# Gated one-hot rows of the PEER gates: from VectorE and ScalarE to GpSimd

## What is computed

```python
q = (xt @ w_query).reshape(T, PEER_HEADS, 2, HALF_Q)
scores = jnp.einsum('thpc,hpnc->thpn', q, sub_keys)
top_s, top_i = lax.top_k(scores, PEER_TOPK)
# the best 16 of the 16 x 16 sums of both halves: idx = i0 * 128 + i1
gate = jax.nn.softmax(best_s, axis=-1)
act = jax.nn.gelu(jnp.einsum('cd,ced->ce', xc, expert_u[ic]), approximate=False)
y = jnp.einsum('ce,ced->cd', gc * act, expert_v[ic])
```

## Time and profile before

| | |
|---|---|
| median of three runs | 3446.96 us (3443.82 to 3449.16) |
| profiled execution | 3449.76 us |
| its span | 3447.9 us |
| mean granted TensorE clock | 0.947 |
| instructions | 51796 |
| HBM read | 663.03 MB |

### The profile page before, as it was taken

One profiled execution on the slowest core, in us unless ns is written; L12 is line 12 of the kernel. 1 busy time (PEld: TensorE's weight loads), 2 busy tenths in 40 slices (PEclk: granted clock), 3 DMA queues, 4 the chain that ended last, 5 costly groups with the idle time before them and its releaser, 6 DMA issues.

```text
span 3447.9 us, 51796 instructions
## 1 busy us (share of the span) xinstructions
PE 3063.0 (89%) x18029; PEld 2438.0 (71%) x18029; DVE 1839.0 (53%) x3381; ACT 1275.3 (37%) x2062; POOL 38.0 (1%) x77
## 2 busy tenths in 40 slices
PE   6979997997999776999996999988699999689997
PEld 4763443783444756999985788877599999568885
DVE  3532222624221465697459555556559944975555
ACT  0111111021111362444447545436344444655443
POOL 0000000000000100000000000010000000000000
PEclk9989998997999868999999999987799999999998
DMA  8647996653999311445540455532135545025552
GB/s 338 269 171 295 421 421 268 256 219 136 421 421 376 112 49 74 170 174 181 182 146 0 159 185 191 183 122 101 49 135 183 183 176 183 19 100 192 183 185 95
DMA packets 91679, 665.76 MB, mean 193 GB/s; under 512 B 10336, under 2 KB 10336, under 8 KB 10656
## 3 DMA queue, kind: packets, MB, share of 16 engines
q1 hardware_dynamic: 90864, 660.65, 50.0%
q0 software_dynamic: 544, 2.42, 0.2%
q10 hardware_dynamic: 144, 1.05, 0.1%
HBM read 663.03 MB, written 1.05 MB: 193 GB/s over the span
## 4 chain that ended last, share of the span: by engine, by line
PE 73%; DVE 12%; DMA 7%; issue 4%; ACT 2%; DVEq 2%; SPq 0%; ACTq 0%
PE acc L549 21%; PE lin L549 18%; PE duo L549 9%; DMA arena<-w_moe 7%; PE lin L510 6%; PE lin L723 5%; PE duo L754 3%; DVE arena L1922 3%; PE duo L499 2%; PE duo L510 2%; PE acc L768 2%; DVE hot L1915 1%; PE acc L583 1%; DVE w_lo L1335 1%; DMA arena<-w_ada 1%
## 5 line engine op out<-in xcount | busy, mean ns | idle before, releaser
L1335 DVE TENSOR_TENSOR w_lo<-slot,w_hi 128x1024 fp32r<-128x1024 f32 x608 | 742.3, 1223 | 384.6 <-ACT w_hi L1001 381.3
L1001 ACT ACTIVATE w_hi<-slot 128x1024 fp32r<-128x1024 f32 x608 | 643.4, 1059 | 623.1 <-PE acc L549 353.5
L549 PE MATMUL lin<-x_parts,w_hi 128*128 128x256 f32 x3584 | 477.0, 286 | 74.1 <-DVE x_parts L1665 74.1
L549 PE MATMUL acc<-w_hi,x_parts 128*128 128x512 f32 x2048 | 521.6, 397 | 1.6 <-ACT x_parts L1004 1.6
L549 PEld LDWEIGHTS lin<-x_parts,w_hi 128*128 128x128 f32 x3584 | 454.6, 192 | 77.4 <-issue 77.3
L549 PEld LDWEIGHTS acc<-w_hi,x_parts 128*128 128x128 f32 x2048 | 386.0, 189 | 96.1 <-ACT x_parts L1004 2.6
L723 PE MATMUL lin<-arena 128*64 128x512 f32 x1248 | 313.5, 601 | 20.0 <-DMA arena<-w_moe 17.1
L549 PE MATMUL acc<-w_lo,x_parts 128*128 128x512 f32 x1024 | 281.5, 397 | 0.0
L1332 DVE TENSOR_TENSOR x_parts<-arena,x_parts 128x256 fp32r<-128x256 f32 x256 | 108.9, 425 | 317.7 <-ACT x_parts L1004 317.7
L549 PE MATMUL lin<-x_parts,w_lo 128*128 128x256 f32 x1792 | 253.3, 284 | 0.8
L723 PEld LDWEIGHTS lin<-arena 128*64 128x64 f32 x1248 | 110.5, 137 | 189.4 <-issue 142.0
(11 more groups left out here) (347 smaller groups left out, 2933.1 us busy)
## 6 DMA issues: line engine op xcount, KB each, us to landing
slot<-wstream SPq DMA_DIRECT2D x348, 1024.0 KB, 4.8
arena<-w_moe SPq DMA_DIRECT2D x234, 1024.0 KB, 16.6
arena<-w_ada SPq DMA_DIRECT2D x28, 1024.0 KB, 8.9
ada_home<-w_ada SPq DMA_DIRECT2D x20, 1024.0 KB, 7.7
xT<-x_in POOLq DMA_DIRECT2D x1, 1024.0 KB, 9.8
out<-xT ACTq DMA_DIRECT2D x1, 1024.0 KB, 3.9
par<-params POOLq DMA_DIRECT2D x2, 270.0 KB, 9.0
invc<-inv_count POOLq DMA_DIRECT2D x1, 512.0 KB, 14.3
```

Source lines behind the costliest of these rows:

```text
L549: return mm(out_, a, b, start=start, stop=stop)
L1001: last = A(w_hi[c % 2][:, :], slot[j % SLOTS][:, (c % 2) * HALF:(c % 2 + 1) * HALF], ACT.Copy)
L1335: TT(w_lo[c % 2][:, :], slot[j % SLOTS][:, (c % 2) * HALF:(c % 2 + 1) * HALF], w_hi[c % 2][:, :].bitcast(F32), ALU.subtract).then_inc(slot ...
```

## The change

The gated rows are now made by GpSimd, with one instruction for each token that compares `iota` with the first index and multiplies by the gate. Both are operands of one value for each partition. They go where the one-hot rows of i0 lay, `hot[:, g % 3, 0]`; `gated_hot` and `scale_group` are gone, and with them ScalarE's part. VectorE compares for the plain rows alone, 4 x 128 elements a partition. TensorE waits for both sorts of rows. There are three buffers for either sort now, so `g_done` starts at three. GpSimd's program is written out, for both layers and all 64 groups, without loops.

```diff
-        gated_hot = nc.alloc_sbuf_tensor_at("gated_hot", [P, 2, 4, P], F32, offset=REGION + 4 * HOTS * 8 * P)
-        hot_ready, scaled_hot = sem("hot_ready"), sem("scaled_hot")
+        gated_ready, plain_ready = sem("gated_ready"), sem("plain_ready")
@@ GpSimd
-            with pool.Fori(0, L) as l:
+            for l in range(L):
                 pool.wait_ge(layer_end2, l + 1)
                 pool.dma_start(par2[:, 0:NCOL2], params2[l]).then_inc(par2_loaded, 16)
...
+                def gated_rows(g, i):
+                    n = l * G4 + i * 6 + g
+                    pool.wait_ge(g_done, n + 1)
+                    for t in range(4):
+                        at = slice(4 * g + t, 4 * g + t + 1)
+                        last = nc.gpsimd.tensor_scalar(hot[:, g % HOTS, 0, t, :], iota[:, 0:P], picksT[:, 0, at],
+                                                       picksT[:, 2, at], ALU.is_equal, ALU.mult)
+                    last.then_inc(gated_ready, 1)
+
+                pool.wait_ge(ptr_out, l + 1)
+                pool.wait_ge(lin_free, l * UNITS2 + BASE2 + UNITS2 + LB)
+                for g in range(G4):
+                    gated_rows(g, 0)
@@ TensorE
-            pe.sem_inc(g_done, 2)
+            pe.sem_inc(g_done, HOTS)
...
-                    pe.wait_ge(scaled_hot, n + 1)
+                    pe.wait_ge(gated_ready, n + 1)
+                    pe.wait_ge(plain_ready, n + 1)
                     for t in range(4):
-                        last = mm(acc[:, g % HOTS, t * P:(t + 1) * P], gated_hot[:, g % 2, t, :],
+                        last = mm(acc[:, g % HOTS, t * P:(t + 1) * P], hot[:, g % HOTS, 0, t, :],
                                   hot[:, g % HOTS, 1, t, :], start=True, stop=True)
@@ ScalarE
-                def scale_group(g, i):
-                    n = l * G4 + i * 6 + g
-                    act.wait_ge(hot_ready, n + 1)
-                    act.wait_ge(g_done, n + 1)
-                    for t in range(4):
-                        last = A(gated_hot[:, g % 2, t, :], hot[:, g % HOTS, 0, t, :], ACT.Identity,
-                                 scale=picksT[:, 2, bass.ds(i * 24 + (4 * g + t), 1)])
-                    last.then_inc(scaled_hot, 1)
@@ VectorE
-                    TT(hot[:, g % HOTS], iota[:, 0:P].unsqueeze(1).unsqueeze(1).to_broadcast([P, 2, 4, P]),
-                       picksT[:, 0:2, at].unsqueeze(3).to_broadcast([P, 2, 4, P]), ALU.is_equal)\
-                        .then_inc(hot_ready, 1)
+                    TT(hot[:, g % HOTS, 1], iota[:, 0:P].unsqueeze(1).to_broadcast([P, 4, P]),
+                       picksT[:, 1, at].unsqueeze(2).to_broadcast([P, 4, P]), ALU.is_equal)\
+                        .then_inc(plain_ready, 1)
...
-                    dve.wait_ge(g_done, l * G4 + i * 6 + g + 3)
+                    dve.wait_ge(g_done, l * G4 + i * 6 + g + (HOTS + 1))
```

## The result

The changed kernel takes 3646.72 us, the median of four runs (3646.09 to 3647.42), against 3448.06 for the kernel before in the same rounds (3443.82 to 3452.62). The ratio is 1.0576, 95% interval 1.0558 to 1.0594: slower by 198.7 us, where the prediction said 131.8 slower, and inside its range. The profiled execution has a span of 3645.7 us, 197.8 more than before.

The account below looks back on a forecast made before the run. VectorE was taken to bound the gate stage; after the change GpSimd would, with 4 x 0.62 + 0.30 = 2.78 us a group, making each stage 179.9 us instead of 114.0. Two layers add 131.8 us: 3579, range 3458 to 3761.

Parts of the forecast that it names:

- What bounds the kernel: Gate stage: VectorE sets the period of 1.73 us a group; halving its comparison alone would give 1.20.
- break-even: Gate stage: the GpSimd period, 1.75 us a group, below which the change beats the old time.
- The price of one operation: GpSimd's fused operation of 128 elements: 0.62 us taken, between 0.37 and 0.98; four are 2.48 us a group.
- What VectorE takes: Gate stage: GpSimd time lost beside VectorE's two-SBUF-input comparison, 0.30 us a group taken, at most 0.70.
- The clock: TensorE's granted clock in the gate stage may fall to 0.50; cost 0 to 4 us a layer, summed as zero.
- The edits put at nothing: Moved g_done wait, GpSimd's new waits, its longer written-out program and the weight stream: no cost in the sum.
- Rival 3: GpSimd's operation is heavy, comparison and scalars doubling it: 0.90 us each, period 4.0, time 3735; chance 0.20 (period over 3.6).
- Rival 1: GpSimd's operation is light, 0.25 us as an affine select: period 1.30, kernel faster at 3389; chance 0.10.

Follow-up runs that it names:

- memset kernel: The changed kernel, but GpSimd fills each group's gated rows with a constant by one memset of 512 elements instead of four operations (gates wrong): 3375.3 us.
- PSUM run: The changed kernel, but VectorE compares against a copy of iota in PSUM, leaving its comparison one SBUF input: 3625.45 us, ratio to before 1.0513.

## Why the prediction came out as it did

**What bounds the kernel.** Right. The period of the kernel before was VectorE's, and the memset kernel shows that halving its comparison brings exactly the 1.20 us that were worked out. The break-even at a GpSimd period of 1.75 us needs 0.44 us an operation; even the cheapest form measured, one step with an immediate, starts every 0.49 us and took 3509.2 us. So the sign was settled by the 0.49 worked out of the earlier trace rows, and turned only on its lower bound, 0.37, not being the true one.

**The price of one operation.** This is the term that was mis-sized. The base of 0.49 was right to the hundredth. For the second step and the scalars I added 0.13 out of bounds of 0 and 0.49; the runs show 0.28, most of it the second step. Four operations cost 3.09 us, not 2.48. The 0.61 us too little are 39 us a layer, 78 in all, and more than the whole miss of 67. The step that failed was to stay near the row instead of giving the second step a price of its own.

**What VectorE takes.** 0.20 us a group instead of 0.30, 13 us in all too much, and by another rule than I used. Shares of VectorE's time (0.35, 0.75) aren't a property of the engines: only a start inside a comparison is held, until about 0.11 us before that comparison ends, and longer only where others follow at once and the operation reads scalars from memory. That reads back into the rows of before: L469 at 1154.52 keeps its 1.49 us although L1335 begins at 1155.64, L469 at 1156.07 is held, and the affine select at 1158.80 is held for 0.98 of the 1.11 us that L1335 still needs. The first L469, at 1150.88, lasts 2.03 us, held for 0.54 by the first of the pair of L1335 that began at 1150.33, and not by the second, which is the one that gets longer. Short GpSimd operations start often and lose much, long ones little. In the changed kernel the comparison is short and comes once in four starts. The Trainium skill's page "SBUF — State Buffer", section "SBUF: two separate sides", with its exclusive lock in which the loser blocks, agrees where it is GpSimd's operation that comes second. It doesn't agree the other way: VectorE's comparison at 1800.63 begins with 0.59 us of GpSimd's operation left and is longer by only 0.10. The PSUM run agrees with the section "Who interferes with whom" that it takes two SBUF inputs; to price each group with the whole comparison (0.70 us) would have been 0.5 us too much.

**The clock.** Left open, put at zero, and nearly so: it fell to 0.50 within 3 us of the stage's start and stayed there to its end. A group of matmuls then lasts 2.08 us (2.3 forecast), still hidden under 3.27. It shows at the end of the stage, which took 2.9 us behind the last GpSimd operation instead of 2.0, and at the start of the value stage, whose first eight matmul records take 3.00 us instead of 2.14, with a granted clock of 0.69 over 7 us: about 1 us a layer each.

**The sum again.** 210.6 us of GpSimd (64 x 3.09 and 12.7 of holds, 1.5 of them at the first operation, which falls into VectorE's first three comparisons and lasts 2.27 us) and 2.9 of end: 213.5 us, against 179.9 in the prediction. The edits put at nothing cost nothing: no wait of GpSimd's inside the stage, no DMA in it (share 0.00), ScalarE silent for 214 us.

**The rivals.** Rival 3, a heavy operation (period over 3.6), had the right reason, a second step with a price of its own; the measured 3.3 lies between the forecast and it, inside the forecast's own 1.92 to 3.6. Rival 1 was right that a light GpSimd gives VectorE's period (3375 measured with a still lighter GpSimd, 3389 worked out), and failed by GpSimd's price. The Trainium skill's "GPSIMD Engine Reference", section "Engine selection", with one-input operations at roughly line rate, isn't borne out for any tensor-scalar here: 0.49 us for 128 elements at the least.

## What to carry to other kernels

Work moved to an idle engine is free only if that engine's period for it is under the old one: price it from that engine's own rows, with the fixed part and the part for each element apart, and give every further step and operand a price; here the cheap end of the unknown wasn't the one that came. If the operations of two engines hold each other up, look where the starts of the one fall in the operations of the other; a copy of an operand in PSUM can take the clash away, and here it turned a loss of 1.8% into a gain of 0.6%. The slow helper paid here as the maker of every third group, not of all, and only with that copy.

## What was unexpected of the hardware

- Two-step tensor-scalars with immediates on GpSimd cost 0.70 us for 128 elements, one-step ones 0.49; a scalar from memory adds 0.07 to 0.08. On VectorE the fused operation with two scalars costs 0.26.
- Four comparisons of 128 elements in a row hold a GpSimd start for 0.26 us, more than the 0.09 that one of them could, and less than the 0.35 of one long one. In front of three comparisons of 512 elements in a row a GpSimd operation with immediates is held for 0.44 us, with one scalar from memory for 0.97, with two for 1.49.
- TensorE's granted clock, 0.99 in the first gate stage of the kernel before, was 0.50 (the 1.2 GHz level) in the changed kernel, where TensorE waits more than a microsecond for each group. Eight matmul records last 2.08 us there instead of 1.16; the waiting hides it, and only what follows the stage pays, about 1 us.
